# Layer 2 of a three-layer block: differential attention between half tiles of the projection, forgetting attention alone

## What is computed

```
aq, ak, av, af, bq, bk, bv = split_cols(h @ w_in, EVEN_SPLITS)
log_f = log_sigmoid(af + fgate_b)
o_a = fox_attention(aq, ak, av, log_f)      # 8 heads of 64; score + (c_q - c_k), c = cumsum(log_f)
# bq, bk: 4 heads with two maps of 64 each, rotated (partial rope); bv: 4 heads of 128
p1 = softmax(mask(q1 @ k1.T * scale)); p2 = softmax(mask(q2 @ k2.T * scale))
o_b = (p1 - lam * p2) @ bv                  # differential attention
o_b = rms_norm(o_b, subln) * (1 - lam_init)
x = x + concat([o_a, o_b]) @ w_out
```

## Time and profile before

| | us |
|---|---|
| median of 3 runs | 2493.31 |
| lowest and highest | 2484.49, 2494.50 |
| the profiled execution | 2471.22 |
| its span | 2469.4 |

### The profile page before, as it was taken

How to read it: one execution, slowest core, us unless ns; L and a number is a source line. 1 busy time by engine, 2 the same in 40 slices (tenths; PEclk the granted TensorE clock), 3 DMA queues, 4 the chain that set the end, 5 groups by cost and what they waited for, 6 DMA issues and landing times. The chain is left out here.

```text
span 2469.4 us, 32541 instructions
## 1 busy us (share of the span) xinstructions
PE 2298.5 (93%) x11705; PEld 1858.7 (75%) x11705; DVE 1342.2 (54%) x2258; ACT 865.8 (35%) x1354; POOL 814.3 (33%) x387
## 2 busy tenths in 40 slices
PE   4998998899999999899879999999898799999998
PEld 4777986778788888778657788877676557888877
DVE  4587655477704772423673577721497563677601
ACT  3425212433322332332353333322323563433322
POOL 2000000344443444376103344443463004344442
PEclk8999998899999999999888999999999899999999
DMA  3320000223332333233002233333331003233332
GB/s 117 94 77 1 1 2 25 75 80 92 101 101 79 93 102 103 73 85 85 26 1 60 78 101 96 92 90 97 75 92 52 1 1 94 77 102 93 90 93 81
DMA packets 345821, 177.68 MB, mean 72 GB/s; under 512 B 16639, under 2 KB 343418, under 8 KB 345722
## 3 DMA queue, kind: packets, MB, share of 16 engines
q1 hardware_dynamic: 344122, 175.24, 24.6%
q10 hardware_dynamic: 1056, 1.06, 0.1%
q0 software_dynamic: 544, 0.06, 0.0%
HBM read 174.23 MB, written 2.11 MB: 71 GB/s over the span
## 5 line engine op out<-in xcount | busy, mean ns | idle before, releaser
L294 POOL TENSOR_TENSOR wlo<-raw,whi 128x1024 fp32r<-128x1024 f32 (+2 forms) x319 | 743.5, 2335 | 1540.2 <-ACT whi L290 894.0
L307 PE MATMUL banks<-xhi,whi 128*128 128x512 f32 x1712 | 682.6, 399 | 5.1 <-DVE cb L1030 3.9
L308 PE MATMUL banks<-xlo,whi 128*128 128x512 f32 x1712 | 670.3, 392 | 0.0
L309 PE MATMUL banks<-xhi,wlo 128*128 128x512 f32 x1712 | 669.9, 391 | 0.0
L307 PEld LDWEIGHTS banks<-xhi,whi 128*128 128x128 f32 x1712 | 324.1, 189 | 84.0 <-issue 13.5
L308 PEld LDWEIGHTS banks<-xlo,whi 128*128 128x128 f32 x1712 | 324.0, 189 | 71.4 <-issue 5.3
L309 PEld LDWEIGHTS banks<-xhi,wlo 128*128 128x128 f32 x1712 | 323.7, 189 | 68.3
L871 ACT ACTIVATE whi<-raw 128x1024 fp32r<-128x1024 f32 (+1 forms) x216 | 209.8, 981 | 187.1 <-DMA raw<-in_ffn_w_out_dram 84.2
L959 ACT ACTIVATE cb<-banks,conv 128x512 f32<-128x512 f32 x152 | 118.0, 779 | 446.2 <-DVE banks L1019 446.2
L307 PE MATMUL banks<-ghi,whi 128*128 128x512 f32 x608 | 238.8, 393 | 19.8 <-DVE xT L1061 13.8
L308 PE MATMUL banks<-glo,whi 128*128 128x512 f32 x608 | 237.2, 390 | 0.0
(11 more groups left out here) (448 smaller groups left out, 2798.6 us busy)
## 6 DMA issues: line engine op xcount, KB each, us to landing
raw<-in_ffn_w_in_dram SPq DMA_DIRECT2D x88, 512.0 KB, 3.8
raw<-in_w_ffn_up_dram SPq DMA_DIRECT2D x64, 512.0 KB, 4.0
raw<-in_w_ffn_down_dram SPq DMA_DIRECT2D x32, 512.0 KB, 4.4
raw<-in_ev_w_in_dram SPq DMA_DIRECT2D x25, 512.0 KB, 3.9
raw<-in_ffn_w_out_dram SPq DMA_DIRECT2D x32, 384.0 KB, 3.6
raw<-in_ffn_w_out_dram SPq DMA_DIRECT2D x32, 320.0 KB, 3.3
raw<-in_od_w_in_dram SPq DMA_DIRECT2D x20, 512.0 KB, 3.6
raw<-in_w_in_dram SPq DMA_DIRECT2D x19, 512.0 KB, 3.8
```

Source lines behind the costliest of these rows:

```text
L294: return pool.tensor_tensor(wlo[c][:, 0:n, :], raw[b][:, 0:n, :], whi[c][:, 0:n, :].bitcast(F32), ALU.subtract)
L307: pe.matmul(acc, whi[b][:, k, :], hi(k), start=first and k == 0, stop=False)
L308: pe.matmul(acc, whi[b][:, k, :], lo(k), start=False, stop=False)
L309: mm = pe.matmul(acc, wlo[b][:, k, :], hi(k), start=False, stop=last and k == n - 1)
```

## The change

- The order of the projection's tiles is new: bq and bk in turn (tiles 0 to 7), bv (8 to 11), af (12), av, aq, ak (13 to 24).
- `project` with `EvenSide` is replaced by a stage written out (`enter_even`). VectorE evicts each tile with the multiplication in one instruction. Rotations follow tiles 6 to 13, transposes of bv tiles 12 and 13, transposes of av (through bank 7) tiles 18 to 21; ScalarE copies the transposes.
- From tile 14 on each tile is cut in two halves of the depth, and TensorE does one step of the differential attention behind each half. It has one pair of score banks, one transpose bank, two output banks, and two `ex` buffers instead of four.
- The running sums of the forget gates are stored in memory and read back spread over the partitions, in four transfers of two heads each.
- The forgetting attention (`fox`) is a stage of its own with one output bank. The norm of the differential output is in it: squares and root ahead of ScalarE's first exponential, the sums behind TensorE's first score, spreading and multiplication in steps 1 to 4. Its two instructions per tile became one.
- `project_out` is the same work; `Cut` and `project_out` got a parameter with the old value as default.

```diff
-    in_ev = [tile_of(we, c0) for c0 in [1536] + [o + 128 * m for o in (1024, 0, 512, 2568, 1544, 2056) for m in range(4)]]
+    in_ev = [tile_of(we, c0) for c0 in [o + 128 * m for m in range(4) for o in (1544, 2056)] + [2568 + 128 * m for m in range(4)] + [1536]
+             + [o + 128 * m for o in (1024, 0, 512) for m in range(4)]]
...
+        at = Attention(ctx, units, [(2, 3)], [4], [5, 6], lam=lam, buffers=2)
+        START = 14
...
+            for m in range(N):
+                load(sp, s0 + LOADED + m)
+                if m == 18:
+                    sp.wait_ge(spreading.h, 1)
+                    sp.dma_start(forgets[:, :], w).then_inc(stored.h, 16)
+                if 19 <= m < 23:
+                    h = 2 * (m - 19)
+                    if h == 0:
+                        sp.wait_ge(stored.h, 16)
+                    sp.dma_start(f[:, h:h + 2, :], bass.AP(tensor=forgets.tensor, offset=h * S, ap=[[0, P], [S, 2], [1, S]])).then_inc(stored.h, 16)
...
+                    dense(m, 0, KD // 2)
+                    if step(m, 0) == 0:
+                        pe.wait_ge(free.h, 12)
+                        pe.wait_ge(rot.used.h, 8)
+                    if step(m, 0) == at.FLIP:
+                        pe.wait_ge(vb_taken.h, NT)
+                    if step(m, 0) >= 0:
+                        at.pe(pe, step(m, 0))
+                    dense(m, KD // 2, KD).then_inc(w_used.h, 1)
+                    if step(m, 1) >= 0:
+                        at.pe(pe, step(m, 1))
...
+                if A0 + 5 <= m < A0 + 9:
+                    t = m - A0 - 5
+                    pe.wait_ge(free.h, A0 + 4)
+                    if t:
+                        pe.wait_ge(va_taken.h, t)
+                    for q in range(4):
+                        mm = pe.transpose(bank[7][:, q * P:(q + 1) * P], av[:, q, t * P:(t + 1) * P], ident)
+                    mm.then_inc(va_turned.h, 1)
...
+                for half in range(2):
+                    if step(m, half) >= 0:
+                        at.act(act, step(m, half))
+                if m == AF + 3:
+                    act.wait_ge(made.h, 1)
+                    chain(act.activation(y, af[0:NH, :], ACT.Abs))
+                    chain(act.activation(y, y, ACT.Exp, scale=-1.0))
+                    act.activation(y, y, ACT.Ln, bias=1.0).then_inc(did.h, 1)
+                if A0 + 6 <= m < A0 + 10:
+                    t = m - A0 - 6
+                    act.wait_ge(va_turned.h, t + 1)
+                    act.activation(vta[:, t, :, :].rearrange("p m n -> p (m n)"), bank[7][:, :], ACT.Copy).then_inc(va_taken.h, 1)
...
+                if step(m, 0) >= 0:
+                    at.dve(dve, step(m, 0))
+                dve.wait_ge(w_used.h, s0 + m + 1)
+                free.by(dve.tensor_tensor(dst[m], bank_of(m), rs, ALU.mult))
+                if step(m, 1) >= 0:
+                    at.dve(dve, step(m, 1))
...
+            at = Attention(ctx, units, [(0, 1), (2, 3)], [4, 5], [6])
...
+                    if 1 <= i < 5:
+                        k = i - 1
+                        pe.wait_ge(inverted.h, 1)
+                        if k:
+                            pe.wait_ge(finished.h, k + 1)
+                        for t in range(NT):
+                            mm = pe.matmul(bank[7][:, t * P:(t + 1) * P], st[:, 2, 4 * t + k:4 * t + k + 1].broadcast_to([P, P]), ident, start=True, stop=True)
+                        mm.then_inc(spread.h, 1)
```

More of the change, by code:

```diff
@@ L262, in _program @@
     for layer in range(2):
-        plan += (in_ev, in_od)[layer] + [tile_of((woe, wod)[layer], 128 * m) for m in range(8)]
+        plan += (in_ev, in_od)[layer]
+        plan += [tile_of((woe, wod)[layer], 128 * m) for m in range(8)]
         plan += up_slots(wu2[layer], FF2, 0, 22) + down_slots(wd2[layer], 0, PARTS2)
@@ L646, in pe @@
                 pe.wait_ge(self.got.h, 16)
-            if n >= 3:
-                pe.wait_ge(self.used.h, n - 2)
-            pe.matmul(bank[4 + n % 3][:, :], self.sw[:, :], x, start=True, stop=True).then_inc(self.swapped.h, 1)
+            if n >= len(self.banks):
+                pe.wait_ge(self.used.h, n - len(self.banks) + 1)
+            pe.matmul(bank[self.banks[n % len(self.banks)]][:, :], self.sw[:, :], x, start=True, stop=True).then_inc(self.swapped.h, 1)
         def dve(self, dve, x):
@@ L655, in dve @@
                 dve.wait_ge(self.turned.h, 2 * n - 2)
-            self.used.by(dve.tensor_tensor(self.t[:, n % 2, :], bank[4 + n % 3][:, :], self.sinT[:, :], ALU.mult))
+            self.used.by(dve.tensor_tensor(self.t[:, n % 2, :], bank[self.banks[n % len(self.banks)]][:, :], self.sinT[:, :], ALU.mult))
             self.turned.by(dve.tensor_tensor(x, x, self.cosT[:, :], ALU.mult))
@@ L1083, in __init__ @@
             self.J = 1 if lam is not None or self.joined else 2
-            self.ex = [sb(ctx, f"ex{i}", [P, 2, widest]) for i in range(4)]
+            self.NE = buffers
+            self.ex = [sb(ctx, f"ex{i}", [P, 2, widest]) for i in range(buffers)]
             self.pt = [sb(ctx, f"pt{i}", [P, 2 * widest if self.joined else widest]) for i in range(2 * self.J)]
@@ L1125, in pe @@
                     for g, b, at in self.flat(u, j):
[L1126 removed]
+                        mm = pe.transpose(bank[self.t_banks[n % len(self.t_banks)]][:, at:at + P], self.ex[u % self.NE][:, g, b * P:(b + 1) * P], ident)
                     mm.then_inc(self.flipped.h, 1)
@@ new lines, in even_mixer @@
+    def even_mixer(oT, f):
+        lam_init = 0.8 - 0.6 * math.exp(-0.3 * 0)
+        with ExitStack() as fx:
+            aq, ak = (sb(fx, n, [P, 4, S]) for n in ("aq", "ak"))
+            vta = sb(fx, "vta", [P, NT, 4, P])
+            ident_r, mask_r = sb(fx, "ident_r", [P, P], F32R), sb(fx, "mask_r", [P, P], F32R)
+            with ExitStack() as pr:
+                bq, bk = (sb(pr, n, [P, 4, S]) for n in ("bq", "bk"))
+                vtb, mask, lam = sb(pr, "vtb", [P, NT, 4, P]), sb(pr, "mask", [P, S]), sb(pr, "lam", [P, 1])
+                enter_even(pr, f, bq, bk, oT[:, 4:8, :], vtb, aq, ak, oT[:, 0:4, :], vta, oT[:, 4:8, :], mask, ident_r[:, :], mask_r[:, :],
+                           lam[:, 0:1], lam_init)
+            close_feed()
+            fox(aq, ak, vta, f, oT, ident_r, mask_r, lam_init)
@@ L2397, in layers @@
                 open_feed()
-                project_out(oT, ("ffn_norm", KD * layer))
+                if layer == 0:
+                    project_out(oT, ("ffn_norm", 0))
+                else:
+                    project_out(oT, ("ffn_norm", KD))
             ffn(wu2[layer], FF2, wd2[layer], conv2[layer], 0, 22, PARTS2, ACT.Silu, True, xT, lambda ctx, y: Ready(ctx),
```

321 lines of the change are left out of this document (185 added, 136 removed).

## The result

| | before | after |
|---|---|---|
| median, us | 2492.07 | 2506.56 |
| lowest and highest | 2484.49, 2494.50 | 2504.39, 2510.69 |
| the profiled execution's span | 2469.4 | 2502.3 |
| TensorE busy | 2298.5 (93%) | 2316.0 (93%) |
| VectorE busy | 1342.2 (54%) | 1347.2 (54%) |

The changed kernel takes 1.0065 times as long as the one before (95% interval 1.0039 to 1.0092), so it is slower, by 14.5 us between the medians. The time lies in my range of 2474 to 2508, but I had called "no change" the likeliest and forecast 2492.

A forecast was written before the change was run, and what follows sets the result against it. Attention and norm stages were held to run at the pace of a loop between engines, the projection by TensorE; 33 + 24.5 - 59.2 = -1.7 us gave 2469.5 profiled, forecast as a 2492 median, range 2474 to 2508.

The forecast's parts named there:

- Projection: Layer 2's projection: tiles 6 to 13, with rotations and transposes, end at 1119.8 us, before the differential attention's steps begin.
- The attention's own work on TensorE: Differential attention between the projection's half tiles: 7.6 us a head, 30 for four, nearer 28 without short waits.
- rival 4: Half tiles wait for VectorE or ScalarE; attention adds 43.2 us instead of 30; total 2502; chance 0.08.
- The turns' waits: Projection tiles 19 to 21: TensorE waits for ScalarE's copy of transposed forgetting values, 3.6 + 2.5 + 3.6, say 10 us.
- The wait at the gate: Projection, tile 15: forget gate's instructions and table loads delay ScalarE's copy, so the transpose bank waits 2 us.
- The closed loop: Forgetting stage: with one bank each value product waits for VectorE's previous store; 18.1 us a head instead of 11.7.
- the first rival: Forgetting stage: the one bank is hidden, heads keep 11.7 us, stage takes 60, total 2468; chance 0.11.
- The sum: Projection plus 33, forgetting stage plus 24.5, removed differential attention and norm stages minus 59.2: -1.7 us.
- The stage, 83 forecast: Forgetting stage with the norm inside: 83 us at clock 0.85 against 58.6, plus 24.5; ends 75 and 92.
- The 75: Forgetting stage at full clock: step 5 starts at 17, steps 5 to 7 13.8, two heads 36.2, end 8.
- The projection, +33 forecast: Path to the forgetting stage: it starts at 1227 us instead of 1194, with 2 us allowed for lower clock.
- Rival 3: Forgetting stage: TensorE's clock stays low for most of it; stage 103 us, total 2511; chance 0.17.

The follow-up runs named there:

- run 3: Changed kernel with two output banks in the forgetting stage and ScalarE's copies of the forgetting values ahead of its attention steps: 2461.46 us, 0.9883 of the kernel before.
- run 7: Changed kernel with differential attention in its own stage, two output banks and ScalarE's forgetting-value copies ahead of its other work: 2468.22 us, 0.9912 of the kernel before.
- run 2: Changed kernel with ScalarE's copies of the forgetting values moved ahead of its two attention steps in a tile: 2498.85 us, 1.0034 of the kernel before.
- run 4: Changed kernel with two unused 512-column matmuls ahead of each value product in steps 6 to 15 of the forgetting stage: 2501.55 us, one execution.
- run 1: Changed kernel with the forgetting stage's value products alternating between two PSUM banks from unit 2 on: 2473.47 us, 0.9936 of the kernel before.
- run 9: Changed kernel, one output bank kept, with VectorE's store first in each step of the forgetting attention: 2471.32 us, 0.9934 of the kernel before.
- run 8: Kernel before with only the forgetting attention's output banks cut from two to one: 2517.29 us, 1.0111 of the kernel before.
- run 5: Changed kernel with the norm as its own stage ahead of the forgetting attention, one output bank kept: 2518.94 us, 1.0127 of the kernel before.

## Why the prediction was right or wrong

**Right.**
- Projection: the last tile before the attention ends at 1118.6 us on before's time axis (1136.2 less the 17.6 of layer 1), forecast 1119.8. The eviction on VectorE and, behind that tile, the sums through memory cost TensorE nothing: none of its waits over 0.25 us is ended by a transfer or an eviction.
- The attention's own work on TensorE, 30 us: 28.6 by runs 3 and 7. That half tiles would wait for VectorE or ScalarE (rival 4) didn't happen.
- The turns' waits, 3.6 + 2.5 + 3.6: measured 3.69, 2.49 and 4.06, each ended by ScalarE's copy. (The four pieces of the first, 3.1, 1.07, 0.3 and 0.6, add up to 5.1 and not to 5.2.) Run 2 shows that the place of that copy behind the two attention steps made them. The wait at the gate, 2: measured 2.28.
- The closed loop: TensorE's waits ended by the store in nearly every step, 18.1 us a head at full clock; 18.06 in run 4. The mechanism is shown from three sides: another bank (run 1), another order (run 9), and the kernel before with the bank taken away (run 8).
- The loop is there without the norm too (runs 5 and 8), and the first rival, that one bank would be hidden, is out. The Trainium skill's rule to rotate independent groups through PSUM banks ("Perfetto Trace Analysis", "Matmuls") agrees with run 1; run 9 adds that one bank is enough where it is emptied in time. The remark in the Trainium skill ("TensorE: Matmul & The Clock Gate", "HAM oscillation") that double-buffering gave no further gain, made of another kernel, doesn't carry over to this one: the second bank is worth 30.5 us in run 1, and the measurement decides.

**Wrong: the size of two terms.** The sum gave the mixer -1.7 us, and it took 15.6 more. The terms were all there; 13.4 of the difference are in the term for the forgetting stage and 3.8 in that for the projection.
- *The stage, 83 forecast, 96.5 measured.* I had 75 at full clock and added 8, for a clock of 0.85 read from the neighbouring stages of the kernel before (0.77 and 0.88). This is the step that failed: the clock assumed for the new loop, and the head of the stage placed by hand.
  - *The clock.* TensorE is busy 87% and 79% of those two stages, and by my own working it would wait for VectorE's stretch in each step of the new loop; the clock there was 0.69. Run 4 gives the price. Up to the sixth score's minimum the two kernels are alike (23.9 and 23.8 us). Then after takes 16.2 us to the next head's first minimum, 23.1 for that head and 33.4 for the last one and the end; run 4, at full clock for most of that, takes 15.1, 18.1 and 28.1. The differences, 1.1 + 5.0 + 5.3, are 11.4 us, where I had allowed 8.
  - *The 75.* The other 10 us are in run 4 too: the sixth minimum at 23.8 instead of 18.3 (step 5 at 17, and 1.3 for its score), three steps at 15.1 instead of 13.8, and 28.1 for the last head and the end instead of 24.8. Run 9 tells what most of the first is: with the store moved, the sixth minimum comes at 20.2. So 3.7 of these 5.5 us are the closed loop itself, which begins in step 4, where the norm's last spreading stands behind the waiting product (VectorE idles 3.05 us at 1270.9 in after); I had let it begin in step 5. The first exponential came 7.6 us after the stage's start, forecast 5.4, which can be the rest: the sixteen column sums took 5.1 us, at a clock of 0.52 from 1251.2 to 1254.3, where four times 0.81 would be 3.2 at the full one. What the last 1.3 and 3.3 us are, the low clock (0.69 in run 4's drain) or the working, isn't shown.
- *The projection, +33 forecast, +36.8 measured.* Behind the turns' waits the clock fell and stayed low for some microseconds. I added 2 "between 0 and 5"; run 2 makes it 6.1.

Rival 3 named the low clock and gave it 0.17, with 103 us for the stage and 2511 in all. What happened lies between it and the forecast, past the 92 us that I had called the stage's upper end; that the time still lies in the range is due to the width of the range and not to the sum. Rival 3 deserved more: the norm stage of before, a chain of short pieces between engines like the new loop, was at 0.68; I named it for the rival and took the clock of the two attention stages for the sum.

**The balance.** The removed stages give 59.2 us. The projection takes 36.8 of them: 28.6 for the attention, 12.5 waits, 6 clock, less some 10 that the spreads and the tail had cost. That leaves 22.4. The forgetting stage then takes 37.9, of which 33.3 are the place of one VectorE instruction, so long as there is one bank (run 9), or 30.5 the missing bank (run 1). With the bank the mixer would have been 14.9 us shorter than before (run 1), and with the early copies too 29.9 (run 3).

**What stays open.** Why the clock of layer 1 differs between executions, which is worth 17 us, isn't known. Why loops of the same instructions ran at different clocks (heads of 23.1 us in after and of 23.9 in run 5, the stages of after and run 2) isn't known. A filling of TensorE wasn't tried in the stages' heads, where the clock is 0.65 to 0.79 even in the best versions.

## What to carry to other kernels

When a pipeline loses a buffer, write one step of each engine's list side by side and see where the release of the buffer stands: moving the release to the head of the list can be worth as much as a second buffer. Work out a new loop's length at both clocks, and where TensorE waits in every step of it, let the low one carry the forecast unless a row shows a like loop at the full one. Work placed between dense matmuls costs the dense engine its whole length, 28.6 us here, so the move earned 11 of the 45 us that the work took in a stage of its own. The waits that the move brought were paid twice, in idle time and in clock.

## What was not expected of the hardware

- Adding work made a stage shorter: 20 matmuls (40 records, 18.8 us busy) took it from 96.5 to 85.1 us. The granted clock was 1.00 while they ran, where it is 0.69 in the loop of after.
- Taking the norm out of the stage didn't make the loop faster: its clock was 0.63 over the attention's stage (run 5), and a head took 23.9 to 24.0 us instead of 23.1 to 23.6.
- Waits of 2.5 to 4 us within dense work cost more than themselves: 10.2 us of waiting in three places came with 6.1 us of low clock (run 2).
- 16 matmuls of one column (32 records), back to back, 5.9 us long and with no gap between them, ran while the granted clock went down; ahead of them lay the change of stage, with 1 us of idle time in 2. Windows of run 3, ahead of them and from their start on:

```profile
1234.00:1236.00 2.00, 0.95 (x8) 0.54 (x6) 0.84 (x2) 0.65 (x2) 0.00 (x0) 1.00 0.00 0
1236.00:1240.00 4.00, 4.00 (x26) 4.00 (x25) 0.51 (x4) 2.82 (x4) 0.00 (x0) 0.65 0.00 0
1240.00:1244.00 4.00, 4.00 (x18) 3.33 (x18) 0.65 (x3) 1.76 (x3) 0.00 (x0) 0.50 0.00 0
```
